# A two-layer decoder step: order of the first loads, place of the value pages, and where squares are added

## What is computed

```python
def decoder_layer(x, c, ...):
    m = (jax.nn.silu(c) @ cond_w + cond_b).reshape(c.shape[0], 9, 1, 1024)
    def pre(i, h):
        return rmsnorm(h, norm_pre[i]) * (1.0 + m[:, 3 * i + 1]) + m[:, 3 * i]
    def post(i, h, y, rw):
        return h + rw * m[:, 3 * i + 2] * rmsnorm(y, norm_post[i])
    x = post(0, x, swiglu(pre(0, x), ffn_w_in[0], ffn_w_out[0]), 0.5)
    o, ... = mixer(pre(1, x), mix_w_in, mix_w_out, ...)
    x = post(1, x, o, 1.0)
    x = post(2, x, swiglu(pre(2, x), ffn_w_in[1], ffn_w_out[1]), 0.5)
```

## Time and profile before

| | us |
|---|---|
| median of 3 runs | 1559.38 |
| lowest, highest | 1558.02, 1560.41 |
| the profiled execution | 1558.12 |
| its span | 1556.6 |
| PE busy in it | 1410.2 (91%) |
| DVE, ACT busy | 808.2 (52%), 591.9 (38%) |

### The profile page before, as it was taken

The page is one execution under the profiler, slowest core; times in us unless marked ns, Lnnn a source line. Parts: engine busy times, 40 slices in busy tenths (PEclk is TensorE's granted clock), DMA queues, the critical chain, the costliest instruction groups (busy, mean ns, idle before and its releaser), DMA issues.

```text
span 1556.6 us, 36279 instructions
## 1 busy us (share of the span) xinstructions
PE 1410.2 (91%) x13900; PEld 1315.3 (84%) x13900; DVE 808.2 (52%) x1186; ACT 591.9 (38%) x954; POOL 56.4 (4%) x130
## 2 busy tenths in 40 slices
PE   4699999989976899999979999998997779999997
PEld 3599999888954779999969999997996567999996
DVE  2344543557882365554364455345789336455434
ACT  2322333533433352333453333334345335233344
POOL 3000000100021000000000000001002100000000
PEclk9699999999988899999979999999998979999998
DMA  7687574899948496554557857569995759765453
GB/s 241 214 279 246 162 240 147 245 302 277 302 162 272 142 341 193 165 161 134 162 165 240 276 164 225 175 198 335 266 318 171 255 160 339 212 167 166 122 164 106
DMA packets 432308, 335.12 MB, mean 215 GB/s; under 512 B 16131, under 2 KB 356387, under 8 KB 432172
## 3 DMA queue, kind: packets, MB, share of 16 engines
q1 hardware_dynamic: 429900, 327.65, 68.7%
q0 software_dynamic: 2272, 5.61, 1.1%
HBM read 328.41 MB, written 4.78 MB: 214 GB/s over the span
## 4 chain that ended last, share of the span: by engine, by line
PE 78%; DVE 6%; SPq 5%; DMA 4%; ACT 3%; issue 2%; DVEq 2%; ACTq 0%
PE PS L550 20%; PE PS L552 19%; PE PS L551 19%; PE PS L574 4%; DMA direct<-in_cond_w 3%; PE PS L595 3%; PE PS L597 2%; PE PS L596 2%; SPq L427 2%; PE PS L773 1%; SPq L448 1%; PE PS L922 1%; PE PS L819 1%; DVE direct L1713 1%; DMA direct<-in_cache_sb_v 1%
## 5 line engine op out<-in xcount | busy, mean ns | idle before, releaser
L1505 DVE TENSOR_TENSOR w_lo<-raw,w_hi 128x1024 fp32r<-128x1024 f32 (+1 forms) x372 | 396.9, 1107 | 563.4 <-ACT w_hi L1171 563.4
L1171 ACT ACTIVATE w_hi<-raw 128x1024 fp32r<-128x1024 f32 (+1 forms) x372 | 339.9, 960 | 756.5 <-PE PS L552 650.3
L550 PE MATMUL PS<-a_hi,w_hi 128*128 128x288 f32 x1664 | 498.8, 300 | 0.0
L551 PE MATMUL PS<-a_lo,w_hi 128*128 128x288 f32 x1664 | 490.9, 295 | 0.0
L552 PE MATMUL PS<-a_hi,w_lo 128*128 128x288 f32 x1664 | 489.3, 294 | 0.0
L550 PEld LDWEIGHTS PS<-a_hi,w_hi 128*128 128x128 f32 x1664 | 311.9, 187 | 8.2 <-issue 7.5
L552 PEld LDWEIGHTS PS<-a_hi,w_lo 128*128 128x128 f32 x1664 | 313.3, 188 | 0.0
L551 PEld LDWEIGHTS PS<-a_lo,w_hi 128*128 128x128 f32 x1664 | 312.4, 188 | 0.5
L550 PE MATMUL PS<-h_hi,w_hi 128*128 128x288 f32 x704 | 215.0, 305 | 8.3 <-DVE w_lo L1505 8.3
L552 PE MATMUL PS<-h_hi,w_lo 128*128 128x288 f32 x704 | 209.9, 298 | 0.0
L551 PE MATMUL PS<-h_lo,w_hi 128*128 128x288 f32 x704 | 209.2, 297 | 0.0
(11 more groups left out here) (295 smaller groups left out, 1249.0 us busy)
## 6 DMA issues: line engine op xcount, KB each, us to landing
...
direct<-in_cache_sb_k SPq DMA_DIRECT2D x128, 256.0 KB, 4.2
direct<-in_cache_sb_v SPq DMA_DIRECT2D x128, 256.0 KB, 4.0
...
```

The lines of the kernel that those rows point to most:

```text
L550: pe.matmul(out, whi, hi, start=begins and i == 0, stop=False)
L551: pe.matmul(out, whi, lo, start=False, stop=False)
L1171: act.activation(w_hi[:, s, at_:at_ + n], raw[:, s, at_:at_ + n], ACT.Copy)\
L1505: tt(w_lo[:, s, at_:at_ + n], raw[:, s, at_:at_ + n], w_hi[:, s, at_:at_ + n], ALU.subtract).then_inc(lo_done.sem, 1)
```

## The change

It has five parts.

1. Start. The rows c and two condition chunks are issued first on SP, then x, two more chunks, the page table, four chunks, and the first two weight steps last. The vectors (`vrow`) are loaded by seven transfers on ACT's queue instead of fourteen on SP's. `rows_in` is replaced by `c_in`, `x_in`, `vrow_in` and `pages_in`; the identity has a signal of its own. PE uses chunks 0 and 1 before it turns x, 2 and 3 before the squares of x. Four of eight first scalings go from ACT to DVE, and the first splits stand behind them on DVE; the fourth half is split in `pre`, also where layer 1 begins (`seam_post` of k = 2 then splits one half, not two).
2. Nine condition chunks instead of five are loaded within w_out of FFN 0.
3. All value pages are issued before the weights of `mix_w_out`. ACT copies `sample_rows(1)` before it waits for `outs_done`, and `sample_heads(1)` between two half splits.
4. Squares. In an FFN DVE adds blocks 0 to 5 of the squares into a cleared `ysq` block (`add_squares`); PE sums that one and the blocks 6 and 7: 3 matmuls, not 8. In the mixer DVE adds the pairs of steps 0 to 2 into `yacc`; 4 matmuls, not 8.
5. ACT adds to `yb_free` after each of the last two silus.

```diff
-            sp.dma_start(pages[:, :], page_table.rearrange("b n -> (b n)").unsqueeze(0)).then_inc(rows_in.sem, 16)
-            sp.dma_start(ctok[0:1, :], c_prompt).then_inc(rows_in.sem, 16)
...
+            sp.dma_start(ctok[0:1, :], c_prompt).then_inc(c_in.sem, 16)
+            sp.dma_start(ctok[1:NC, :], c_sample).then_inc(c_in.sem, 16)
+            for s in range(2):
+                cond_load(0, 0, s)
             for i in range(PT_):
...
+            for s in range(2, 4):
+                cond_load(0, 0, s)
+            sp.dma_start(pages[:, :], page_table.rearrange("b n -> (b n)").unsqueeze(0)).then_inc(pages_in.sem, 16)
+            for s in range(4):
+                sp.wait_ge(direct_used.sem, 4 + s + 1)
+                cond_load(0, D, s)
             for s in range(2):
                 ffn_in(0, 0, s, s)
...
-                for i in range(2 if n == 0 else 0):
+                for i in range(3 if n == 0 else 0):
                     for s in range(4):
                         ffn_out(l, n, i * 2 + s // 2, s % 2, s % 2, i * 4 + s)
-                        if i * 4 + s < 5:
+                        if i * 4 + s < 9:
                             cond(l, 2, i, s)
...
-                cond_seam(l, 2, 5, 12)
+                cond_seam(l, 2, 9, 12)
...
                 for n in range(NPC):
-                    if n == NPC - 2:
-                        sp.wait_ge(ds_sum.sem, ds_sum.at(l, GP))
-                        sp.sem_inc(raw_free.sem, 1)
-                        for s in range(2):
-                            mix(l, mix_w_out, POS_MO, s, s, s * 256)
                     page_chunk(l, cache_sb_v, DP_V, 4 * n, n, n)
+                sp.wait_ge(ds_sum.sem, ds_sum.at(l, GP))
+                sp.sem_inc(raw_free.sem, 1)
+                for s in range(2):
+                    mix(l, mix_w_out, POS_MO, s, s, s * 256)
...
-                        if s == 1 and not first:
-                            squares(i * 2 - 1, 1)
-                        if s == 3:
-                            squares(i * 2, 0, begins=first)
+                        if s == 2 and last:
+                            pe.wait_ge(y_summed.sem, y_summed.at(l, 2 * n + 1))
+                            pe.matmul(PS[:, 5, 0:T], ones[:, :], ysq[:, 2, :], start=True, stop=False)
+                        if s == 3 and last:
+                            squares(i * 2, 0)
...
                     silu(N_IN - 2 + s, s)
-                act.drain()
-                act.sem_inc(yb_free.sem, 2)
+                    act.drain()
+                    act.sem_inc(yb_free.sem, 1)
...
+                sample_rows(1)
                 act.wait_ge(outs_done.sem, outs_done.at(l, 1))
-                split(l, POS_MO, 0, 0)
-                sample_rows(1)
+                split(l, POS_MO, 0, 0, only=(0,))
                 sample_heads(1)
+                split(l, POS_MO, 0, 0, only=(1,))
...
-                split(*after, 0, 1, only=(0,) if k < 2 else (0, 1))
+                split(*after, 0, 1, only=(0,))
...
+                def add_squares(m, s):
+                    dve.drain()
+                    dve.wait_ge(yb_free.sem, yb_free.at(l, YB_OUT[n] + 3) + m)
+                    return tt(ysq[:, 2, :], ysq[:, 2, :], ysq[:, s, :], ALU.add)
...
+            for kb in range(KB // 2, KB):
+                ts_(Y[:, kb, 0:NP], X[:, kb, 0:NP], M[:, 0, KB + kb, 0:1], None, ALU.mult)
             scale_samples(0)
+            split(0, POS_IN[0], 0, 0)
+            split(0, POS_IN[0], 0, 1, only=(0,))
```

154 lines of the change are left out of this document (90 added, 64 removed).

## The result

The kernel after takes 1521.05 us (median of 4 runs, 1519.65 to 1526.87), beside it the kernel before 1559.89: the ratio is 0.9755, 95% interval 0.9722 to 0.9787. Run again beside other executions of before it was 1520.21 (6 runs), ratio 0.9709 (0.9685 to 0.9733). The profiled span went from 1556.6 to 1518.6 us, 38.0 less. The sum had promised 62.5. The direction was right; the time lies 24 us above the forecast of 1497 and 5 us above the upper end of its range.

A forecast was written before the change was run, and what follows sets the result against it. TensorE stood on the path for 78% of the span, so only removable PE work and PE gaps counted. The terms summed to 62.5 us off 1558.12, giving 1495.6, as median 1497; range 1480 to 1516.

The forecast's parts named there:

- 1. Start: Start of the kernel: first product at 45 us instead of 59.35, 14.4 us less, bounds 8 and 18.
- (b): Start bound by PE at half clock: chunk 7 used at 40, first product at 51; 1503 us; chance 0.10.
- (e): Chunk loads held by slots PE frees, not queue place, so start and seam stay; 1516 us; chance 0.05.
- 2. and 3. FFNs: Four FFNs: waits from w_in to w_out go, 8.9 us less; fewer square sums on PE, 9.7 less.
- rival (d): Additions on DVE wait for ACT's squares and delay the next split; slower, about 1608 us; chance 0.03.
- Step 3: Squares in w_out steps: fewer square sums on PE, 9.7 us less in the FFNs, 3.9 in the mixer.
- Term 6: Layer turn: one split leaves DVE's queue, 1.8 us less once; seam after the mixer 0.3 per layer more.
- Rival (c): Supply: weights and chunks come no faster, so the FFN squares' 9.7 and seam's 4.8 are lost; 1511; chance 0.07.
- 4. Nine chunks: Seam before the mixer: four more chunks loaded within w_out, 2.4 us less per layer, 4.8 in all.
- a longer wait there: Far side of the seam before the mixer: PE's wait for turned keys longer than 1.7 us.
- Rival (a): Mixer's end: stores move with the traffic, outs_done 4 us later, each layer gains 5.8 only; 1505; chance 0.10.
- term 5: Mixer's end: value pages before w_out weights, first product 510.7 against 520.51; 9.8 us less per layer, 19.6.

The follow-up runs named there:

- b3: The kernel after with the FFN output's squares summed on TensorE again, one product per output block, VectorE's additions kept; 1531.1 us, ratio to before 0.9763.
- b4: The kernel after with ScalarE again telling TensorE of both free PSUM banks at once, behind the second SiLU; 1531.0 us, ratio to before 0.9793.
- c2: The kernel after with five instead of nine condition chunks fetched inside w_out, the other seven in the seam; 1530.1 us, ratio to before 0.9779.
- b2: The kernel after with the fifth mix_w_in chunk issued between the second and third key page chunk, not behind the fourth; 1514.9 us, ratio to before 0.9662.
- a0: The kernel after run again unchanged; 1520.2 us, ratio to before 0.9709.
- d2: The kernel after without stores of k rows and sample state, and with both half splits of mix_w_out's first chunk ahead of the sample heads; 1512.5 us.
- a5: The kernel after with both half splits of mix_w_out's first chunk ahead of the sample heads' work; 1514.7 us, ratio to before 0.9685.
- a3: The kernel after without the stores of k rows and sample state and without the waits for them; 1516.7 us, ratio to before 0.9697.
- b1: The kernel after with four cond_w chunks issued ahead of the third and fourth chunk of mix_w_out; 1515.3 us, ratio to before 0.9675.

## Why the prediction was wrong

**1. Start: right.** 15.4 for 14.4. PE is through with the last chunk at 32.4 instead of 34, as the clock was 1.00 from 20 to 30 us where the forecast took a mixed one; the splits behind it took 11.5 instead of 11. Rivals (b), with the first product at 51, and (e), with the start unchanged, are out. The term was read from two traces and not undone alone.

**2. and 3. FFNs: right.** 17.8 for 18.6, confirmed by b3 and b4 one by one. PE's waits have none on `w_lo` and none on the additions, so rival (d) is out.

**3. Mixer: right in size (4.2), wrong in worth.** Step 3 took every product in a busy stretch as time. Behind the output stands a seam whose transfers end at their own time: between the first wait and its end the DMA engines are full. The forecast asked what is late next in the FFNs and at the mixer's end, but not here. Term 6 had 0.3 us per layer for seam 2; it was 1.7 and 4.2. Rival (c), supply, named this mechanism, but put it at the FFN and at seam 1, where it did not strike.

**4. Nine chunks: undersized.** Seam 1 itself gained 1.5 per layer where the term had 2.4 with all that follows; c2 shows that the same edit saves 5 per layer once the rest of the change is in. Its effect was worked out on the old timetable. What it hands on to the mixer is lost in the key wait (4.75 and 4.34), which is gone in b2: a weight chunk was queued behind four key chunks, with DVE standing at its split. The forecast had named a longer wait there as a sign, and put none of it into the body. The body's 3.7 us in layer 1 is hardly more than the 3.2 that a0 shows from one trace to the next.

**5. Mixer's end: the step that failed.** 5.0 for 19.6. The forecast had the last page chunk in time, so that `outs_done` would end last. It was the other way round: the stores ended where they had been (27.6 us behind the landmark, 27.9 before), ScalarE never waited for them, and PE waited 5.13 us for the page chunk, where the forecast's own sign was a wait below 2. From the landmark to the use of the last page chunk the forecast had 24.5 us (501 less 476.5), measured 28.9 in layer 0. The stores make 2.1 of these 4.4 (d2: 26.8, with the chunk issued at the same place). From the last issue to the use of the chunk there are 7.8 us in the kernel after, 8.6 in a0 and 8.7 in a5, but 5.1 in a3 and 6.2 in d2, without the stores. Of the other 2.3, the chunk's first issue came 0.7 later (18.95 us behind the landmark for 18.2), and the other 1.6 are the rows' own time: d2 takes 7.9 us from this issue to the use, where the forecast had 6.3 from an assumed rate and landing time. In other runs the first issue came at 21.0 instead of 18.95, and the chunk about as much later.

The first product then came 12.2 us behind the chunk's use, not 9.7. Before had both half splits done (505.07 to 507.07) ahead of the last chunk's work. The new order has the first behind the copy of the rows and the second behind the heads' copy, for which ScalarE first waits 2.29 us. The forecast listed that very queue, but took the transposes as done and left this wait out; a5 fills it and takes 2.0 us off. With 2.1, 2.3 and 2.0 the 6.9 missing in layer 0 are accounted for up to 0.5. For layer 1 (7.6 missing) a3, a5 and d2 show the same two terms; the rest is not divided further. Rival (a) had stores and traffic in it, but let `outs_done` be late, which it was not.

**Of the sum as a whole:** 14.6 of the 25 missing us are term 5, 5.3 seam 2, 5.4 seam 1 with the body. Rival (e) at 1516 was no bound: the range counted each term's own uncertainty, but not that the stages behind take gains back, which hits all terms in front of a seam at once.

Open: why the last page chunk is issued 19 us behind the landmark in some traces and 21 in others; why seam 2 shows a half-clock stretch in some traces and not in others at similar waits; and the worth of b1, b2 and a5 each by itself.
